# Gate norm sums as two rounded matmuls of head and rest, and the two heads of an indexer pair taking turns, in a four-layer transformer kernel

## The reference

```
yg = (y * jax.nn.silu(z.astype(jnp.float32))).reshape(b, L, g, SSD_NORM_GROUP)
yg = yg * lax.rsqrt(jnp.mean(yg * yg, -1, keepdims=True) + RMS_EPS)
yg = yg.reshape(b, L, SSD_D_INNER) * norm_g
return yg.astype(x.dtype) @ w_out
```

```
s = jnp.einsum('bthd,bsd->bths', qi.astype(jnp.float32), k_idx_f)
score = jnp.einsum('bths,bth->bts', jax.nn.relu(s), wi) * idx_scale
```

## Time and profile before

| what | value |
|---|---|
| time before, median of 3 runs | 2430.32 us (2429.73 to 2431.71) |
| the profiled execution's own time | 2429.53 us |
| its span, first to last instruction | 2428.3 us |
| TensorE (PE) busy | 2417.4 us |
| VectorE (DVE) busy | 1572.8 us |
| ScalarE (ACT) busy | 1243.5 us |
| granted TensorE clock, mean | 1.000 |

### The profile page before, as it was taken

One profiled execution on the slowest core, in us unless ns is written; L12 is line 12 of the kernel. 1 busy time (PEld: TensorE's weight loads), 2 busy tenths in 40 slices (PEclk: granted clock), 3 DMA queues, 4 the chain that ended last, 5 costly groups with the idle time before them and its releaser, 6 DMA issues.

```text
span 2428.3 us, 45481 instructions
## 1 busy us (share of the span) xinstructions
PE 2417.4 (100%) x19626; PEld 2340.7 (96%) x19626; DVE 1572.8 (65%) x2109; ACT 1243.5 (51%) x1426; POOL 88.4 (4%) x68
## 2 busy tenths in 40 slices
PE   9999999999999999999999999999999999999998
PEld 9999999999999999999988899999999999999998
DVE  6778888866577766665575556656654555555556
ACT  5446665554454565554464445445444446455463
POOL 0001000100031000000000000000000000000002
PEclk9999999999999999999999999999999999999999
DMA  8666656557755655547767666666655576555645
GB/s 248 195 197 183 215 182 186 182 189 244 227 173 164 192 165 152 158 151 244 222 195 237 196 198 192 189 185 193 184 189 187 190 234 208 183 174 174 190 158 182
DMA packets 267434, 467.93 MB, mean 193 GB/s; under 512 B 18955, under 2 KB 70497, under 8 KB 265313
## 3 DMA queue, kind: packets, MB, share of 16 engines
q1 hardware_dynamic: 267233, 465.02, 62.0%
HBM read 452.18 MB, written 4.26 MB: 188 GB/s over the span
## 4 chain that ended last, share of the span: by engine, by line
PE 97%; DVE 1%; ACT 0%; DMA 0%; issue 0%; SPq 0%; ACTq 0%
PE G L703 91%; PE M L703 5%; PE M L716 1%; DMA RAW<-in_ssd_w_in 0%; DMA WS<-in_a_w_s 0%; DVE W1m L1547 0%; DVE W L1547 0%; DVE TT L2268 0%; DVE W2m L1547 0%; DVE W0m L1547 0%; DVE E L1640 0%; ACT W L1126 0%; ACT W0m L1126 0%; DVE RES L2263 0%; DVE E L1681 0%
## 5 line engine op out<-in xcount | busy, mean ns | idle before, releaser
L703 PE MATMUL G<-AA,W 128*128 128x256 f32 x7908 | 939.0, 277 | 1.1 <-DVE W L1547 1.0
L703 PEld LDWEIGHTS G<-AA,W 128*128 128x128 f32 x7908 | 915.7, 188 | 5.7 <-issue 2.7
L1547 DVE TENSOR_TENSOR W<-RAW,W 128x1024 fp32r<-128x1024 f32 x446 | 556.8, 1251 | 365.6 <-ACT W L1126 364.4
L1126 ACT CAST W<-RAW 128x1024 fp32r<-128x1024 f32 x446 | 464.9, 1047 | 463.2 <-PE G L703 454.0
L703 PE MATMUL G<-AA,WY 128*128 128x256 f32 x2508 | 304.3, 277 | 0.0
L703 PEld LDWEIGHTS G<-AA,WY 128*128 128x128 f32 x2508 | 293.0, 188 | 1.7 <-issue 1.4
L1547 DVE TENSOR_TENSOR WY<-RAW,WY 128x1024 fp32r<-128x1024 f32 (+1 forms) x112 | 142.2, 1272 | 74.1 <-ACT WY L1126 74.1
L703 PE MATMUL G<-W0m,YY 128*128 128x256 f32 x1512 | 183.7, 276 | 0.4 <-DVE W0m L1547 0.2
L703 PE MATMUL G<-W1m,YY 128*128 128x256 f32 x1512 | 183.1, 276 | 0.3 <-DVE W1m L1547 0.2
L703 PE MATMUL G<-W,YY 128*128 128x512 f32 x792 | 181.3, 389 | 0.0
L703 PE MATMUL G<-W2m,YY 128*128 128x256 f32 x1488 | 180.4, 276 | 0.0
(11 more groups left out here) (306 smaller groups left out, 2397.3 us busy)
## 6 DMA issues: line engine op xcount, KB each, us to landing
RAW<-in_a_w_in SPq DMA_DIRECT2D x192, 512.0 KB, 3.9
RAW<-in_ssd_w_in SPq DMA_DIRECT2D x160, 512.0 KB, 4.4
RAW<-in_b_w_in SPq DMA_DIRECT2D x128, 512.0 KB, 4.1
RAW<-in_dsa_w_in SPq DMA_DIRECT2D x72, 512.0 KB, 3.7
RAW<-in_ssd_w_out SPq DMA_DIRECT2D x64, 512.0 KB, 4.6
RAW<-in_dsa_w_out SPq DMA_DIRECT2D x64, 512.0 KB, 4.2
RAW<-in_a_w_out SPq DMA_DIRECT2D x64, 512.0 KB, 3.8
RAW<-in_b_w_out SPq DMA_DIRECT2D x32, 512.0 KB, 3.8
```

Source lines behind the costliest of these rows:

```text
L703: return e.matmul(o, l, r, start=start, stop=stop, skip_group_check=True)
L1126: e.copy(wh[:, 0:n], RAW[:, v % NR, 0:n]).then_inc(*up(cast_done, "cast", v))
L1547: e.tensor_tensor(wl[:, 0:n], RAW[:, v % NR, 0:n], wh[:, 0:n].bitcast(F), ALU.subtract).then_inc(*up(rest_done, "rest", v))
```

## The change

In the gate norm the one float32 matmul of the folded squares with ones becomes two rounded ones. ScalarE copies the ones once into a rounded tile `ONS`, and for each group writes the rounded head of the folded squares; VectorE writes the rest; TensorE multiplies both by `ONS` and adds. TensorE's sum, ScalarE's root and VectorE's inverse each stand one step later than before; the scaling and what follows stay in their steps. In the indexer the four matmuls of a unit are written in another order: the first products of both heads, then the second products of both heads.

```diff
-LINES = {"CQ": MOVING, "CK": MOVING, "Wx7": STILL, "SPH": MOVING, "SPL": MOVING, "TGR": STILL, "ONR": STILL}
+LINES = {"CQ": MOVING, "CK": MOVING, "Wx7": STILL, "SPH": MOVING, "SPL": MOVING, "TGR": STILL, "ONR": STILL, "SQR": MOVING, "ONS": STILL}
...
+        ("SQR", [P, 2, T], R), ("ONS", [P, P], R)])
...
         def gate_z(g):
-            for _ in range((13, 11)[g > 0]):
-                yield
-            yield
+            for _ in range((15, 13)[g > 0]):
+                yield
             b = take("gs", g)
-            e.wait_ge(*on("fold", g))
-            ones_sum(M[:, b, 0:T], SZ[:, 0, :]).then_inc(*up(pe_made, "gs_m", g))
+            if g == 0:
+                e.wait_ge(*on("ons"))
+            e.wait_ge(*on("sq_rest", g))
+            mm(M[:, b, 0:T], ONS[:, :], SQR[:, 0, :], True, False)
+            mm(M[:, b, 0:T], ONS[:, :], SQR[:, 1, :], False, True).then_inc(*up(pe_made, "gs_m", g))
             yield
...
         def index():
             for h0 in range(0, 16, 2):
+                f, halves = h0 // 2, []
                 for h in (h0, h0 + 1):
-                    f, o = h // 2, 64 * (h % 2)
-                    b = take("is", h)
-                    if h == 0:
-                        e.wait_ge(*on("qi", 0))
-                        e.wait_ge(*on("qi", 1))
-                        e.wait_ge(*on("ki"))
-                    qh = QI[o:o + 64, f // 4, f % 4, :]
-                    mm(M[:, b, 0:P], qh[:, 0:P], KI[o:o + 64, 0:P], True, True)
-                    mm(M[:, b, P:P + T], qh[:, P:T], KI[o:o + 64, :], False, True).then_inc(
-                        *up(pe_made, "is_m", h))
+                    o = 64 * (h % 2)
+                    halves.append((h, M[:, take("is", h), :], QI[o:o + 64, f // 4, f % 4, :], KI[o:o + 64, :]))
...
+                for h, to, q, k in halves:
+                    mm(to[:, 0:P], q[:, 0:P], k[:, 0:P], True, True)
+                for h, to, q, k in halves:
+                    mm(to[:, P:P + T], q[:, P:T], k, False, True).then_inc(*up(pe_made, "is_m", h))
                 yield
...
             e.activation(sz, yv, ACT.Square).then_inc(*up(act_made, "ysq", g))
             yield
             yield
+            if g == 0:
+                e.wait_ge(*on("ones"))
+                e.copy(ONS[:, :], ones[:, :]).then_inc(*up(act_made, "ons"))
+            else:
+                e.wait_ge(*on("gs_m", g - 1))
+            e.wait_ge(*on("fold", g))
+            e.copy(SQR[:, 0, :], SZ[:, 0, :]).then_inc(*up(act_made, "sq_head", g))
+            yield
             yield
             yield
             e.wait_ge(*on("gs_m", g))
...
                          bias=eps6[:, 0:1]).then_inc(*up(act_made, "read", "gs", g))
-            yield
             yield
             e.wait_ge(*on("yn", g))
...
         def gate_z(g):
-            for _ in range((15, 13)[g > 0]):
-                yield
+            for _ in range((14, 12)[g > 0]):
+                yield
+            e.wait_ge(*on("sq_head", g))
+            rest(SQR[:, 1, :], SZ[:, 0, :], SQR[:, 0, :]).then_inc(*up(dve_made, "sq_rest", g))
+            yield
+            yield
             e.wait_ge(*on("read", "gs", g))
             e.reciprocal(RI[:, :], RI[:, :]).then_inc(*up(dve_made, "ri", g))
-            yield
             e.wait_ge(*on("ri", g))
```

More of the change, by code:

```diff
@@ L289, in region @@
         return made
-    BT, CT, XGB, CSB, E2, XD, YT, SZ, CB, RI, dtT, csT = region([
+    BT, CT, XGB, CSB, E2, XD, YT, SZ, CB, RI, dtT, csT, SQR, ONS = region([
         ("BT", [P, 8, T], F), ("CT", [P, 8, T], F), ("XG", [P, 2, 4, T], F), ("CSB", [P, 8, T], F),
         ("E2", [P, 8, 384], F), ("XD", [P, 2, 512], F), ("YT", [P, 4, T], F), ("SZ", [P, 4, T], F),
-        ("CB", [P, 384], F), ("RI", [P, T], F), ("dtT", [P, 2, 64], F), ("csT", [P, 2, 64], F)])
+        ("CB", [P, 384], F), ("RI", [P, T], F), ("dtT", [P, 2, 64], F), ("csT", [P, 2, 64], F),
+        ("SQR", [P, 2, T], R), ("ONS", [P, P], R)])
     RES2, GH2 = region([("RES2", [P, 2, DM], F), ("GH2", [P, 3, 4, P], F)])
@@ L945, in index @@
             for h0 in range(0, 16, 2):
+                f, halves = h0 // 2, []
                 for h in (h0, h0 + 1):
-                    f, o = h // 2, 64 * (h % 2)
-                    b = take("is", h)
-                    if h == 0:
-                        e.wait_ge(*on("qi", 0))
-                        e.wait_ge(*on("qi", 1))
-                        e.wait_ge(*on("ki"))
-                    qh = QI[o:o + 64, f // 4, f % 4, :]
-                    mm(M[:, b, 0:P], qh[:, 0:P], KI[o:o + 64, 0:P], True, True)
-                    mm(M[:, b, P:P + T], qh[:, P:T], KI[o:o + 64, :], False, True).then_inc(
-                        *up(pe_made, "is_m", h))
+                    o = 64 * (h % 2)
+                    halves.append((h, M[:, take("is", h), :], QI[o:o + 64, f // 4, f % 4, :], KI[o:o + 64, :]))
+                if h0 == 0:
+                    e.wait_ge(*on("qi", 0))
+                    e.wait_ge(*on("qi", 1))
+                    e.wait_ge(*on("ki"))
+                for h, to, q, k in halves:
+                    mm(to[:, 0:P], q[:, 0:P], k[:, 0:P], True, True)
+                for h, to, q, k in halves:
+                    mm(to[:, P:P + T], q[:, P:T], k, False, True).then_inc(*up(pe_made, "is_m", h))
                 yield
```

## The result

The changed kernel takes 2442.36 us (median of 5 runs, 2441.51 to 2443.71) against 2430.32 of the kernel before, measured again beside it (5 runs, 2428.60 to 2431.80): ratio 1.0048, interval 1.0036 to 1.0060, 12.0 us slower. The profiled execution took 2441.88 us, its span is 2440.6 and its granted clock 0.999.

A forecast was written before the change was run, and what follows sets the result against it. TensorE was taken to bound the kernel, in step with a ScalarE and VectorE loop that the change lengthens. 2429.53 + 10.8 (gate norm) + 0 (indexer) = 2440.3; median 0.8 above, said as 2441.0; 8-in-10 range 2435.5 to 2444.5.

The forecast's parts named there:

- What bounds, and the loop: Gate norm: ScalarE and VectorE's chain becomes 50.90 us a group against TensorE's 49.15; each of groups 1 to 5 adds 1.75.
- Fold to scaling: Gate norm, from the fold's end to the next scaling: 9.80 us, where it was 8.04.
- scaling to fold: Gate norm, from one group's scaling to the next fold's end: stays at 41.10 us, with nothing there ended by TensorE.
- The rival of a hidden slack: Gate norm loop: unseen slack, each group pays only its own wait; +4.7 us, 2435; chance 0.12.
- The chain ahead of the sum: Behind the fold: head, table load, Silu, cast, weight's rest, rest of squares, ending 5.33 us after it; TensorE waits 0.91.
- The waits for `SQR`: TensorE's sums in groups 1 to 6 each wait for VectorE's rest of the squares, 1.4 to 2.2 us.
- Group 0: First group: no wait for the sum, but the root stands behind one more cast; scaling 1.15 us later.
- Group 6: Its fold is 2.28 us ahead of its sum in place of 1.70, so it adds 1.17 us instead of 1.75.
- All paid at `W1m`: TensorE's unit behind group 6, waiting for VectorE's rest of `W1m`, comes later by all of the chain's 11.1 us.
- The saving of the cheaper sum: TensorE's sum: two rounded matmuls save 0.28 us a group, lost in the wait except in group 7.
- Indexer: Indexer's 8 units: the two heads already run side by side, so the new order gains nothing; units stay at 0.86 us.
- The order rule: Indexer: matmuls start and end strictly in program order, so the turns save 0.2 us a unit, 1.7 in all; chance 0.05.

The follow-up runs named there:

- e6: Kernel before plus one unused VectorE multiplication of 768 columns a group, ahead of the first decays, between scaling and fold: 2436.65 us, 6.0 us slower.
- e7: Changed kernel without the inverse of the root (1.75 us on VectorE a group), behind the sum: gave back 8.9 of the 12 us.
- e3: Changed kernel without head and rest of the squares: float32 sum behind the fold, with sum, root and inverse in their new steps: 2432.67 us.
- e4: Changed kernel with ScalarE writing the head of the squares one step later, behind the Silu and next weight cast: 2432.79 us.
- e5: Changed kernel with head and rest of the squares both made by GpSimd, right behind its fold: 2431.36 us.
- e8: Changed kernel with head and rest on GpSimd, group 6 left as in the kernel before; missed its 2428 target, as two others did, by 4 to 5 us.
- e9: Changed kernel with head and rest on GpSimd and the CSB load issued earlier; missed its 2428 target, as two others did, by 4 to 5 us.
- e10: Changed kernel with head and rest on GpSimd, group 6 as before, CSB load earlier; missed its 2428 target, as two others did, by 4 to 5 us.

## Why the prediction was right, step by step

- **What bounds, and the loop** (the steps that carried it): right. Fold to scaling 10.11 (forecast 9.80), scaling to fold 41.02 (41.10), TensorE's pitch their sum, 51.13 (50.90). e6 and e7 show that it is the loop's length which is paid: each moves the time by an instruction far from the sum. The rival of a hidden slack would have left e6 at 2430.3 to 2431.2; it measured 2436.65.
- **The chain ahead of the sum:** right. Head F + 0.09 to 0.50 (forecast 0.03 to 0.43), rest of the squares to F + 5.41 (5.33), each in the forecast's order. e3 and e4 show that this is the cause: without the head ahead of the Silu, or without head and rest, 10 us are back.
- **Fold to scaling, too short by 0.31:** the rest of the squares ends 0.08 late, `CB` starts at F + 6.72 for 6.60, the inverse at F + 8.33 for 8.14, and the scaling starts 0.04 behind the end of the inverse where I had it overlap by 0.09, as if it were independent. Scaling to fold was 0.08 too long, so the pitch missed by less than its part, 0.23. Groups 1 to 5 lose 5 × 1.98 = 9.9 us for 8.75.
- **The waits for `SQR`:** forecast 1.4 to 2.2 us in groups 1 to 6. They are 1.98 to 2.02 in groups 2 to 5, but 2.46 in group 1 and 1.14 in group 6.
- **Group 0:** no wait for `SQR`, as forecast. The scaling is 200.36 − 198.64 = 1.72 late for 1.15; 0.44 of it is already in the fold, ahead of all that the change touches, and repeated profiles of other kernels put that fold at 189.1 to 191.5 (189.18 before).
- **Group 6:** 1.15 for 1.17. Sum: 1.72 + 9.9 + 1.15 = 12.77 late, for 11.1.
- **All paid at `W1m`:** right, 12.77, with a wait of 1.41 there.
- **The saving of the cheaper sum:** 0.28 forecast for group 7, 12.77 − 12.54 = 0.23 seen up to the indexer. e5 shows it by itself: from the sum of group 0 to that of group 1, with no wait, are 244.22 − 195.37 = 48.85 us for 49.15. In groups 0 to 6 it is gone in the wait, as forecast.
- **Indexer:** right, 0.86 both ways; by itself 0.9998. The order rule of the Trainium skill, TensorE: Matmul & The Clock Gate, Part 3: packing small matmuls, row/col tiling, would have given 1.7 us (0.0007) for it; the ratio's interval includes that, but the unit's 0.86 does not. Nor does the old order's trace agree with the rule, taken by the order in the kernel's text: head B's first product started ahead of head A's second.
- **What showed less than forecast:** ScalarE's idle time ahead of the head is put down to GpSimd, 1.48, but it stands before the cast and not before the table load, because the cast comes first in the list.

The sum was 1.4 us short of the measured 2442.36: 5 × 0.23 = 1.15 from the pitch and 0.57 from group 0, less small differences at the end. One of these is luck: the median is 0.48 above the profiled execution, for the 0.8 that I added. Left open: how much of the 1.27 to 3.0 us that e5, e8, e9 and e10 need more than 294.88 comes from the `CSB` row, the weight transfers and the lateness of either; each has single waits of 1.5 to 2.2 us in its one profile, at other groups in each. A kernel that shortens the loop itself was not tried.

The Trainium skill, Perfetto Trace Analysis, Identifying the Most-Contended Engine, advises to optimize the engine with the highest occupancy first, and judges TensorE by the busy share of its weight loads, among others. By that share, 96%, and by 99 to 100% of matmul time, TensorE is that engine here, and the runs show the limit of it: in this stage a shorter sum on TensorE gave nothing, while 0.95 us in each group on VectorE at 65% cost 6.

## What to carry to other kernels

Where two lightly loaded engines hand work to each other in a ring, measure the ring's length from one landmark to its next occurrence: if it equals the busy engine's pitch, every microsecond put into it is paid once per round, and nothing saved on the busy engine arrives. When a small instruction with a late input is inserted, look at what is queued behind it on its engine: the place in the list (one step, 10 us here) mattered more than the instruction (0.41 us). A cheaper form that needs operands prepared by other engines costs what those wait for, not what they take.

## What the runs showed of the hardware

- GpSimd took 1.21 us for the cast of 256 columns in group 4 of e5_pool, where ScalarE took 0.41, but most of that is VectorE's doing. VectorE's rest of a weight ran until 392.49, and the cast ended 0.26 behind it. In group 7 VectorE is idle, and the same cast takes 0.40. The subtraction, with two inputs, takes 0.74 to 0.75 for VectorE's 0.42.

```profile
535.67 0.40 POOL L2357 CAST SQR<-SZ 128x256 fp32r<-128x256 f32 x1
536.15 0.75 POOL L2359 TENSOR_TENSOR SQR<-SZ,SQR 128x256 fp32r<-128x256 f32 x1
```

- VectorE's rest of 1024 columns takes 1.22 us, but 1.76 when it starts at 394.09 while GpSimd's fold runs until 394.76. It ends 1.09 behind the fold's end. The Trainium skill, SBUF — State Buffer, Who interferes with whom, says that an instruction of VectorE with two inputs in SBUF contends with a GpSimd instruction that reads SBUF, for ports that are held as an exclusive lock, and that the order of issue decides which of the two is blocked. This row agrees, with VectorE blocked.
- The rows beside it agree with the other order. VectorE's rest at 392.96 starts within 0.01 us of the fold and takes its usual time, 1.21; the fold ends 0.60 behind it and takes 1.81 for its 256 columns, more than the 1.31 of the step before it on 512 and the 0.74 of the subtraction above on 256. So by an estimate from these rows about 1 us of the fold, in groups 0 to 6 of both kernels, is time in which VectorE holds GpSimd back. It lies inside the loop. No run here takes it out.
- Two heads of the indexer in separate halves of the rows run side by side whichever way they are written: 0.86 us for a pair in both orders, where the 384 float32 columns of `M<-CT,BT`, as many as one head has, take 0.57 alone.
